# The norm inside a convolution module: another order of its small steps

## The reference

```python
a, g = jnp.split(x @ w_pw1 + b_pw1, 2, axis=-1)
u = a * jax.nn.sigmoid(g)
c, new_buf = _causal_dwconv(u, buf, w_dw, b_dw)      # 31 taps, channel by channel
c = jax.nn.silu(_layer_norm(c, ln_g, ln_b))          # norm over the 1024 channels
return c @ w_pw2 + b_pw2, new_buf
```

## Time and profile before

| | us |
|---|---|
| median of 3 runs | 3036.45 (3036.09 to 3040.01) |
| the profiled execution | 3044.37 |
| its span in the trace | 3042.6 |
| TensorE busy | 2961.6 (97%) |
| VectorE busy | 1678.3 (55%) |
| ScalarE busy | 844.5 (28%) |
| GpSimd busy | 1071.2 (35%) |

### The profile page before, as it was taken

One profiled execution on the slowest core, in us unless ns is written; L12 is line 12 of the kernel. 1 busy time (PEld: TensorE's weight loads), 2 busy tenths in 40 slices (PEclk: granted clock), 3 DMA queues, 4 the chain that ended last, 5 costly groups with the idle time before them and its releaser, 6 DMA issues.

```text
span 3042.6 us, 50077 instructions
## 1 busy us (share of the span) xinstructions
PE 2961.6 (97%) x19348; PEld 2753.5 (90%) x19348; DVE 1678.3 (55%) x2551; ACT 844.5 (28%) x1491; POOL 1071.2 (35%) x742
## 2 busy tenths in 40 slices
PE   7999899999999999999989999999999999999997
PEld 7886889999999998999967878777999999999997
DVE  4877555444444456433457887879327344444445
ACT  4001442222222225111143534434106122222211
POOL 3232123555455523333300101112323346555453
PEclk9999999999999999999989999999999999999999
DMA  8566311111111112433243664848311111111121
GB/s 230 138 150 144 101 32 56 36 41 48 48 55 48 55 30 91 149 113 119 92 172 143 226 225 153 283 149 319 128 43 42 42 56 54 36 41 48 48 76 58
DMA packets 276673, 313.20 MB, mean 103 GB/s; under 512 B 25733, under 2 KB 217477, under 8 KB 275314
## 3 DMA queue, kind: packets, MB, share of 16 engines
q1 hardware_dynamic: 257777, 250.82, 26.8%
q10 hardware_dynamic: 13048, 40.28, 3.4%
q0 software_dynamic: 5712, 20.19, 1.8%
HBM read 219.91 MB, written 92.19 MB: 103 GB/s over the span
## 4 chain that ended last, share of the span: by engine, by line
PE 83%; DVE 5%; DMA 4%; ACT 3%; issue 2%; PEld 1%; POOL 0%; another core or an unknown queue 0%; SPq 0%; ACTq 0%; DVEq 0%; PEldq 0%; POOLq 0%
PE ps L451 20%; PE ps L453 20%; PE ps L452 20%; PE ps L889 4%; PE ps L888 4%; PE ps L890 4%; DMA out_C_s<-CT 2%; PE ps L1529 2%; PE ps L2613 2%; PE ps L1594 2%; DMA CT<-in_state_mlstm_C 1%; PE ps L1550 1%; PE ps L1620 1%; PE ps L1551 1%; PE ps L1552 1%
## 5 line engine op out<-in xcount | busy, mean ns | idle before, releaser
L451 PE MATMUL ps<-AH,WH 128*128 128x352 f32 x3072 | 998.7, 325 | 4.7 <-DVE AL L3135 2.2
L453 PE MATMUL ps<-AH,WL 128*128 128x352 f32 x3072 | 986.0, 321 | 0.0
L452 PE MATMUL ps<-AL,WH 128*128 128x352 f32 x3072 | 985.6, 321 | 0.0
L451 PEld LDWEIGHTS ps<-AH,WH 128*128 128x128 f32 x3072 | 576.8, 188 | 29.9 <-issue 22.6
L452 PEld LDWEIGHTS ps<-AL,WH 128*128 128x128 f32 x3072 | 577.8, 188 | 0.8
L453 PEld LDWEIGHTS ps<-AH,WL 128*128 128x128 f32 x3072 | 577.4, 188 | 0.0
L436 POOL TENSOR_SCALAR WH<-RAW 128x1024 fp32r<-128x1024 f32 x152 | 184.6, 1214 | 947.5 <-PEq L458 700.2
L438 POOL TENSOR_TENSOR WL<-RAW,WH 128x1024 fp32r<-128x1024 f32 x152 | 399.4, 2628 | 12.7
L1112 DVE TENSOR_TENSOR X<-X,ps 128x352 f32<-128x352 f32 x432 | 225.3, 521 | 264.4 <-PE ps L890 133.9
L1003 ACT ACTIVATE SGF<-ps 128x352 f32<-128x352 f32 x192 | 88.9, 463 | 679.7 <-PE ps L453 679.6
L1064 DVE TENSOR_TENSOR HR<-SGF 128x352 f32<-128x352 f32 x144 | 92.8, 644 | 288.4 <-ACT SGF L1003 286.5
(11 more groups left out here) (403 smaller groups left out, 4927.0 us busy)
## 6 DMA issues: line engine op xcount, KB each, us to landing
RAW<-in_ffn_w SPq DMA_DIRECT2D x128, 512.0 KB, 3.7
CT<-in_state_mlstm_C SPq DMA_DIRECT2D x32, 1024.0 KB, 6.8
out_C_s<-CT SPq DMA_DIRECT2D x32, 1024.0 KB, 6.4
RAW<-in_ml_w_in SPq DMA_DIRECT2D x32, 512.0 KB, 3.9
RAW<-in_conv_w_pw SPq DMA_DIRECT2D x24, 512.0 KB, 8.2
STK<-u_scratch SPq DMA_DIRECT2D x64, 184.0 KB, 3.8
xc_scratch<-XC ACTq DMA_DIRECT2D x16, 528.0 KB, 2.7
so_scratch<-SO ACTq DMA_DIRECT2D x16, 528.0 KB, 3.7
```

Source lines behind the costliest of these rows:

```text
L451: pe.matmul(ps[:, bank, 0:CW], wh[:, k, cols], hi[:, k, cs], start=(k == 0), stop=False)
L452: pe.matmul(ps[:, bank, 0:CW], wh[:, k, cols], lo[:, k, cs], start=False, stop=False)
L453: mm = pe.matmul(ps[:, bank, 0:CW], wl[:, k, cols], hi[:, k, cs], start=False, stop=(k == nk - 1))
```

## The change

The norm's small steps are put in another order on four engines, and one of them goes to another engine. `part_no` numbers the partial sums in their new order.

- TensorE: the variance part of chunk 0 and the mean part of chunk 1 come earlier among the last five rows of taps, and the variance sum of chunk 0 before the fifth. The variance part of chunk 1 moves from before the projection to between the products of `pw2(0, 0)`, its sum behind them; those of chunk 2 to `pw2(0, 1)`.
- VectorE: `conv_scale(0)` comes before `ln_center(1)`. The own taps of tile 7 are cut into two pieces of 176 columns for chunks 0 and 1.
- ScalarE: the copy of chunk 2's mean part, then both Silu halves of chunk 0, then the copies to UR, then the square of chunk 1. It no longer rounds.
- GpSimd: rounds each half to AH, behind the four panels of the projection's first half.

```diff
--- before.py
+++ after.py
@@ -475,11 +475,16 @@
         def ln_squares(L):
             return SQC[:, :, ch[2]] if L is ln_c else SQ[:]
 
+        CPART = [(0, 0), (0, 1), (1, 0), (2, 0), (1, 1), (2, 1)]
+
+        def part_no(L, c, m):
+            return L.p + (CPART.index((c, m)) if L is ln_c else 2 * c + m) + 1
+
         def ln_mean_part(pe, L, src, c):
             group_sums(pe, L, 2 * c, lambda k: src[:, k, ch[c]])
 
         def ln_mean_sum(pe, L, c):
-            pe.wait_ge(L.pev, L.p + 2 * c + 1)
+            pe.wait_ge(L.pev, part_no(L, c, 0))
             pe.matmul(ps[:, 2 * c, 0:CW], ones_1[:], partials(L)[:, 0], start=True, stop=True).then_inc(L.mean, 1)
 
         def ln_var_part(pe, L, c):
@@ -487,12 +492,12 @@
             group_sums(pe, L, 2 * c + 1, lambda k: ln_squares(L)[:, k])
 
         def ln_var_sum(pe, L, c):
-            pe.wait_ge(L.pev, L.p + 2 * c + 2)
+            pe.wait_ge(L.pev, part_no(L, c, 1))
             pe.matmul(ps[:, 2 * c + 1, 0:CW], ones_1[:], partials(L)[:, 1], start=True, stop=True).then_inc(L.var, 1)
 
         def ln_part_out(act, L, c, m):
 
-            act.wait_ge(L.part, L.p + 2 * c + m + 1)
+            act.wait_ge(L.part, part_no(L, c, m))
             act.copy(partials(L)[:, m], ps[:, 2 * c + m, 0:CW]).then_inc(L.pev, 1)
 
         def partials(L):
@@ -2477,8 +2482,13 @@
                     split_panel(pool, 4 * i + k, k // 2 + 1 + 2 * i, k, 4 * i + k)
             for k in range(4):
                 if k == 2:
-                    pool.wait_ge(own_tap, tile_taps * (KT - 1) + 4 * len(OWN))
+                    pool.wait_ge(own_tap, tile_taps * (KT - 1) + 6 * len(OWN))
                 split_panel(pool, 16 + k, k // 2 + 9, k, 16 + k)
+            for c in range(3):
+                for m in range(2):
+                    ks = slice(4 * m, 4 * m + 4)
+                    pool.wait_ge(ln_c.y, 2 * c + m + 1)
+                    pool.tensor_scalar(AH[:, ks, ch[c]], CB[:, ks, ch[c]], 1.0, 0.0, ALU.mult, ALU.add).then_inc((ln_c.sig, ln_c.hi)[m], 1)
             for k in range(4):
                 split_panel(pool, 20 + k, k // 2 + 11, k, 20 + k)
             ffn_splits(pool, 0, 0, True)
@@ -2660,8 +2670,7 @@
             pe.wait_ge(sig_done, 3 * KT)
             last_taps(4, {1: lambda: conv_mean_part(0), 3: lambda: ln_mean_sum(pe, ln_c, 0)})
             last_taps(5)
-            last_taps(6, {3: lambda: ln_var_part(pe, ln_c, 0), 4: lambda: conv_mean_part(1)})
-            ln_var_sum(pe, ln_c, 0)
+            last_taps(6, {1: lambda: ln_var_part(pe, ln_c, 0), 3: lambda: conv_mean_part(1), 4: lambda: ln_var_sum(pe, ln_c, 0)})
             ln_mean_sum(pe, ln_c, 1)
             pe.wait_ge(tap_ev, 3 * KT)
             pe.wait_ge(ku_done, KT)
@@ -2669,9 +2678,7 @@
                 mm = pe.transpose(ps[0:HIST + NDEC, 6 + k // 4, (k % 4) * P:(k % 4 + 1) * P], KU[:, k, :], ident[:])
                 if k % 4 == 3:
                     mm.then_inc(t_keep, 1)
-            ln_var_part(pe, ln_c, 1)
             conv_mean_part(2)
-            ln_var_sum(pe, ln_c, 1)
             ln_mean_sum(pe, ln_c, 2)
 
             def pw2(c, u, between=None):
@@ -2694,11 +2701,9 @@
                         between(c, u - 2)
             for c in range(3):
                 for u in range(2):
-                    pw2(c, u)
-                    if c == 0 and u == 0:
-                        ln_var_part(pe, ln_c, 2)
-                    if c == 0 and u == 1:
-                        ln_var_sum(pe, ln_c, 2)
+                    pw2(c, u, (lambda c, n: ln_var_part(pe, ln_c, n + 3)) if c == 0 else None)
+                    if c == 0:
+                        ln_var_sum(pe, ln_c, u + 1)
             ln_pe(pe, ln_m0, lambda c, u, between: pw2(c, 2 + u, between), 2, acc2, 12)
             free_panels(pe, g1_done, G2 + 24, 2)
             ffn_pe(pe, 0, 0, True, False, before=(acc2, 24))
@@ -2868,26 +2873,23 @@
             def conv_half(c, m):
 
                 act.wait_ge((ln_c.aff, ln_c.norm)[m], c + 1)
-                ks = slice(4 * m, 4 * m + 4)
                 for k in range(4 * m, 4 * m + 4):
                     i = act.activation(CB[:, k, ch[c]], CB[:, k, ch[c]], ACT.Silu, bias=PR[:, k, R_CB:R_CB + 1], scale=PR[:, k, R_CG:R_CG + 1])
                 i.then_inc(ln_c.y, 1)
-                act.wait_ge(ln_c.y, 2 * c + m + 1)
-                act.copy(AH[:, ks, ch[c]], CB[:, ks, ch[c]]).then_inc((ln_c.sig, ln_c.hi)[m], 1)
             ln_part_out(act, ln_c, 0, 0)
             act.wait_ge(g1_done, 6 * KT)
             ln_square(act, ln_c, CB, 0)
             ln_part_out(act, ln_c, 0, 1)
             ln_part_out(act, ln_c, 1, 0)
             ln_sqrt(act, ln_c, 0)
-            ln_square(act, ln_c, CB, 1)
+            ln_part_out(act, ln_c, 2, 0)
+            conv_half(0, 0)
+            conv_half(0, 1)
             for q in range(2):
                 act.wait_ge(t_keep, q + 1)
                 act.copy(UR[:, 512 * q:512 * q + 512], ps[0:HIST + NDEC, 6 + q, :]).then_inc(e_keep, 1)
-            conv_half(0, 0)
+            ln_square(act, ln_c, CB, 1)
             ln_part_out(act, ln_c, 1, 1)
-            ln_part_out(act, ln_c, 2, 0)
-            conv_half(0, 1)
             ln_sqrt(act, ln_c, 1)
             ln_square(act, ln_c, CB, 2)
             conv_half(1, 0)
@@ -3028,7 +3030,10 @@
                 pieces = []
                 if lo < SEQ:
                     h = min(hi, SEQ)
-                    pieces.append((CB[:, f, lo:h], lambda t: U[:, s, lo + t:h + t]))
+                    cut = lo + CW // 2 if hi - lo == CW and hi <= SEQ else h
+                    pieces.append((CB[:, f, lo:cut], lambda t: U[:, s, lo + t:cut + t]))
+                    if cut < h:
+                        pieces.append((CB[:, f, cut:h], lambda t: U[:, s, cut + t:h + t]))
                 if hi > SEQ:
                     hist = dec(U[:, s, HIST + SEQ:UW], HIST + DEC_T)
                     pieces.append((dec(CB[:, f, SEQ:TOK], DEC_T), lambda t: hist[:, :, t:t + DEC_T]))
@@ -3133,8 +3138,8 @@
                         dve.wait_ge(d_out, 48)
                     ks = slice(4 * m, 4 * m + 4)
                     dve.tensor_tensor(AL[:, ks, ch[c]], CB[:, ks, ch[c]], AH[:, ks, ch[c]].bitcast(F32), ALU.subtract).then_inc(ln_c.lo, 1)
+            conv_scale(0)
             ln_center(dve, ln_c, CB, 1)
-            conv_scale(0)
             conv_low(0)
             ln_center(dve, ln_c, CB, 2)
             conv_scale(1)
```

## The result

| | before | after |
|---|---|---|
| median, same comparison (7 runs each) | 3038.91 (3036.09 to 3041.25) | 3047.76 (3047.23 to 3053.54) |
| the profiled execution, its span | 3044.37, 3042.6 | 3047.35, 3045.6 |
| mark: pw2(1,0) starts | 339.33 | 346.12 |
| mark: first mean part of the next norm | 389.5 | 397.8 |

The ratio is 1.0027, 95% interval [1.0018, 1.0037]: of 3039 us this is 8.2 us (5.5 to 11.2) on the slower side; the two medians differ by 8.85. Three of the seven runs before are those of the prediction's base (median 3036.45); with four more the median is 3038.91. The forecast was +8.1 us. Why is told behind the experiments.

What follows compares the result with a forecast made beforehand. The chain of waits was taken as the bound, with time to win only where TensorE idles. Front 0, loads and halves 0, variance chain +6.9, clock +1.2 gave +8.1 us: 3044.5 on median 3036.45, range 3037.5 to 3047.

Steps and rivals of the forecast that it cites:

- Chunk 0 gains nothing: First product's second half still waits for UR's landing behind X and starts at 322.25; bounds -1.1 to +0.95 us.
- The variance chain: Chunk 1's variance sum, now behind pw2(0,0), starts its chain later, so pw2(1,0) starts at 346.2 instead of 339.33: +6.9 us.
- Chunk 2 stayed covered: Chunk 2's chain lets pw2(2,0) start at 360.5, before chunk 1's products end at 362.0: cover 1.5 us.
- GpSimd: Rounding of chunk 1's second half takes 1.44 us plus 0.75 for meeting VectorE's subtraction; bounds 0 to 0.9.
- The clock: TensorE's new waits before pw2(1,0) lower its granted clock afterwards: +1.2 us, bounds 0 to 1.6.
- The loads and halved taps: At the convolution's end, full DMA engines keep the last landing and halved taps don't move the end: 0, bounds -2 to +0.5.

Runs made afterwards that it cites:

- with UR first: Changed kernel with UR copied before the Silu halves and its two stores issued ahead of X's loads; 3044.12 us, ratio 1.0018 to the kernel before.
- with the variance early: Changed kernel with chunk 1's variance part and sum moved into the wait before the first product's 13th matmul; 3039.14 us, ratio 0.9997.
- with both: Changed kernel with UR copied early and stored ahead of X, and chunk 1's variance in the first product's wait; 3038.25 and 3038.99 us, ratios 0.9994 and 0.9996.

## Why the prediction was right or wrong

**Chunk 0 gains nothing: right.** The second low half starts at 320.75 (predicted 319.5 to 321.5), the second half of the product at 322.43 (322.25), UR's packets lie behind X's. The prediction took the sentence of the Trainium skill ("DMA: Bandwidth & Descriptors", Queues, rings and completion order) that completion is not first in, first out as leave for UR to land ahead of X. The same section of the Trainium skill says that each DMA engine takes its descriptors in ring order, and the traces agree with that: issued from 308.4 on or at 315.1, UR's rows moved behind X's. X's loads were issued 1.57 us later and not 0.9. That the second half starts within 0.2 us of its old place is partly luck: the bounds were -1.1 and +0.95, and before, this start was released by ScalarE's rounding and not by UR.

**The variance chain: right, step by step.** The sum stands at 331.29, 8.86 behind the second half (8.9). Root done 1.38 behind it (1.34), Silu from 5.42 on (5.3), the rounding of half 1 done at 12.2 (12.3), pw2(1,0) at 14.83 (15.1). The start is 346.12 against 346.2, +6.8 against +6.9. Chunk 2 stayed covered: pw2(1,0) to the next norm takes no wait beyond the clock's.

**GpSimd: right in kind, 0.16 too high.** 1.97 - 1.38 = 0.59 us instead of 0.75. If GpSimd waited for the end of the subtraction, as the Trainium skill has it ("SBUF — State Buffer", SBUF: two separate sides), it would end at 342.23 + 1.38 = 343.61; it ended at 343.45. The rule agrees within 0.16 us.

**The clock: a little low.** Behind pw2(1,0) 1.5 us are lost (51.7 us to the next norm, before 50.2); 1.2 were taken. The whole stage is +8.3 at the next norm.

**The loads and halved taps: right in the sum.** The halves cost 0.633 us a pair against 0.617 (6.33/10 and 6.17/10). The last landing came 0.49 later than in the profile before, which is within the 1.6 us that it scatters among kernels with the same taps. One reading does not hold: the DMA share of 1.07 is that of 285 to 290; over 290 to 297.4 it was 0.77, so that row does not show the engines full up to the landing.

**The step that failed is the last: "on the median of 3036.45 it gives 3044.5".** The change was sized at +8.1 and measured at +8.2 (by the ratio; the medians differ by 8.85); the base was off. Of the 3.3 us between 3044.5 and 3047.76 some 2.5 are the base's. The median of three runs, 3036.45, is low for this kernel: in the comparison its median is 3038.91, in four further sets of runs (17 to 29 each) 3039.95 to 3040.91, and single runs go from 3033.72 to 3049.19. The profiled execution at 3044.37 was a sign of it: the prediction named the 0.26% between the two, and yet gave the base no bound. Laid on 3038.91, +8.1 is 3047.0. The range was built from the bounds of the change's terms alone (3041.5 to 3046, then widened to 3047.0) and had no term for the base; with the 3.6 us from their median to their highest (3040.01) added above, it would have reached 3050.6.

Where does the base scatter? The two profiled spans differ by 3.0 us, though the stage costs 8.3. The same two marks, in the kernel before and after:

```profile
L2717 PE MATMUL ps<-ident,KM x16: 273/273/292, 1547.2 to 1548.8; 128*27 128x128 f32 x16
...
L1471 PE MATMUL ps<-SQH,ones_h x32: 377/379/764, 1642.5 to 2111.8; 128*128 128x256 f32 x32
```

```profile
L2722 PE MATMUL ps<-ident,KM x16: 272/272/293, 1555.5 to 1557.1; 128*27 128x128 f32 x16
...
L1476 PE MATMUL ps<-SQH,ones_h x32: 377/379/634, 1646.9 to 2114.9; 128*128 128x256 f32 x32
```

At 1547 the shift is still 8.3, at the last row sums 3.1. This execution of before took 5.2 us longer for the mLSTM (564.6 instead of 559.4), in code that the change does not touch. These are the two stretches in the columns of the earlier trace rows, before and after:

```profile
1547.20:2111.80 564.60, 534.23 (x3105) 423.19 (x3106) 449.14 (x861) 252.62 (x517) 71.22 (x95) 0.97 0.61 212
```

```profile
1555.50:2114.90 559.40, 528.39 (x3104) 419.79 (x3105) 448.75 (x861) 252.26 (x517) 71.13 (x95) 0.98 0.61 214
```

The same work kept TensorE busy for 5.8 us longer at a granted clock of 0.97 instead of 0.98, while it waited about as long for the state (5.8 and 5.3 us). The base's scatter as a whole goes with the clock: of the 84 single executions of the kernel before whose mean granted clock was taken, the nine at 0.990 have a median of 3044.5 us, the eleven at 0.994 one of 3036.2. Why the clock is low for longer in one execution than in another stays open.

So the shift of a mark right behind the stage is a better measure of the change than the difference of two spans: the next norm is moved by +8.3, +4.9, -0.5 and -2.1 us in the changed kernel, with UR first, with the variance early and with both, and the medians by +8.2, +5.5, -0.9 and -1.8 (ratio less 1, times 3040). The second timing of the kernel with both gives -3.2 and -1.2. For kernels with instructions added on TensorE it does not hold, as told above.

## What to carry to other kernels

A sum that is moved behind a product starts its whole chain there: count the chain from its new start and put it beside the work that is left to cover it. A store whose landing frees memory belongs ahead of loads that nobody awaits yet; here its data were also copied early, and a store ahead of the loads with late data was not tried. Where a forecast is laid on a base, the base's own scatter is a term of the range, best read from all executions that are known, the profiled one too.

## What the hardware showed that was not expected

- Issuing a store right behind three loads (at 308.4) took SyncE 4.15 us instead of 0.36 (at 315.1), and gained nothing in landing. The DMA share was 1.06 in the one case and 1.07 in the other, so full engines alone don't tell them apart; the reason is open.
- 34 instructions added to TensorE's list, hidden in a wait, cost 4 to 8 us some 1250 us later: against the stage's gains of 4.0, 4.1 and 2.4 us stand medians 3.3, 4.0 and 1.8 us above the kernel before (each with an interval of some 3 us to either side). The Trainium skill ("Runtime: NRT & Kernel Launch", Instruction fetch mechanics) says that an engine fetches its instructions through a DMA queue of its own, in blocks. The traces agree: they show such a queue with blocks of 16 KB, and twelve waits for the state have one of its packets beginning inside them, only in the kernels with added instructions. Whether the packet is what holds up the state's load was not tried. An experiment with dummy instructions has this cost in its time; its marks within the stage are to be trusted more.
